# A hybrid encoder layer: the first embedding projection moved into the front stage, routing's order of work changed

## Chip, cores and metric

One core of a Trainium2 chip runs the whole kernel in one launch. The metric is the device time in microseconds; the median of three runs is given for the kernel before.

## What is computed

One layer over 1056 tokens (1024 of a prompt, 32 of a running stream), model width 1024, everything in float32:

```
h  = rmsnorm(x, g_mix);  z = h @ w_in                    # 1024 -> 1536
a  = z_a * sigmoid(z_g);  c = silu(layernorm(dwconv31(a)))
x  = x + concat(c @ w_pw + b_pw, pool_mix(z_u)) @ w_out
h2 = rmsnorm(x, g_ffn)
group = argmax(h2 @ w_rg);  e1, e2 = top 2 of the group's 8 experts (h2 @ w_re)
moe = sum over e1, e2: gate_e * ((silu(h2 @ w_gate[e]) * (h2 @ w_up[e])) @ w_down[e])
x  = x + moe
x  = x + sigmoid(rmsnorm(x, g_ple) @ w_ple_gate + b) * (p @ w_ple_proj)   # p: 256 -> 1024
y  = rmsnorm(x, g_final)
```

There are 32 experts of 6 MB of weights each. The product `p @ w_ple_proj` depends on nothing else in the layer, so it can be computed anywhere before the last stage.

## The kernel before

The 1056 tokens and a gap of 32 rows make nine tiles (`TILES` = 9) of 128 rows. The kernel is written in Bass: every engine has its own hand-written program with semaphores, in four blocks: `front`, `routing`, `experts`, `embedding_gate`. A block ends with a barrier of all engines; below such a place is called a joint.

**`front`** computes everything up to `h2` and the router's logits. Its end is a pipeline over tiles: TensorE's `out_products(t, h)` (the product with `w_out`, half h of the columns), VectorE's `add` and `norm2`, TensorE's `turn2(t, j)` (transposes of `h2`), ScalarE's `h2t_leave`, TensorE's `route(t)` (the logits). SP stores `x2_rows` and `h2_rows` for each tile and, before the last tile, issues the loads of the first expert's six weight pieces (GU 0 to 3, DOWN 4 and 5, 1 MB each) into `raw`. SP's last waits are for the landing of all stores. `p_rows` and `proj_w` are loaded earlier in this stage.

**`routing`** has two strands. VectorE works through a chain of small dependent steps (choice of experts, one-hots, ranks, places in the list of work items), with matmuls of TensorE between them: `count_tokens` and `rank_tokens` after `to_rank` 1, small ones after `to_rank` 2 and 3, and `list_tokens(0)` and `(1)`, which turn `row_parts[0]`, `row_parts[1]` and `at_item` into the list of tokens of each item. GpSimd makes tables of numbers and at the end issues the first gather of tokens. Beside this runs the embedding projection: TensorE's `turn_p(t)` transposes `p`, ScalarE's `leave_p(t)` copies the result out of PSUM, TensorE's `project(t)` multiplies (two halves of two matmuls, each recorded as two), ScalarE's `leave_proj(t)` copies both halves out, and SP's `store(t)` writes them to `proj_rows`. `ps_proj` holds one tile, so a half of `project(t)` waits until `leave_proj(t - 1)` has taken that half; `p_t` and `ps_pt` have two buffers. Tiles 0 to 4 (`LATE` = 5) are projected here, tiles 5 to 8 only turned. ScalarE also makes the six first weight copies (`first_copy`, from `raw` to `work`) and two small Exp steps. SP ends the block with

```
sp.wait_ge(projected, 2 * LATE)
sp.wait_ge(p_turned, T)
for s in (0, 1, 2):
    load_piece(sp, S, s, 1, 1, slice(1, 2))
```

which is two DMA issues for each of three pieces of the second expert.

**`experts`** loops over 49 items (an item is up to 64 tokens of one expert). For each: `gate_up` (32 matmuls), `turn_x` of the next item, `down` of the item before, `turn_hid`. ScalarE and VectorE copy the next expert's pieces from `raw` to `work` when the expert changes; SP loads two experts ahead, as `w_ready` allows, and at the end loads what the last stage needs, ending with `g_final_rows`. **`embedding_gate`** combines, gates and normalises.

Helper lines that the profile shows: L106 is a weight copy, L90 and L94 its loads, L1574 `project`, L1564 `turn_p`, L1519 `leave_p`, L1527 `leave_proj`, L1458 `store`, L1596 `list_tokens`, L1639 VectorE's two-input steps in `routing`, L1303 `route`, L1297 `turn2`, L1938 `turn_x`, L1951 `gate_up`.

## Time and profile before

| | us |
|---|---|
| median of three runs | 1168.76 (1167.81 to 1170.07) |
| profiled execution, its own time | 1167.64 |
| its span, first to last instruction | 1165.9 |
| `front` ends, `routing` begins | 409.8 |
| first transpose of `experts` | 447.95 |
| TensorE busy | 1075.2 (92%) |
| VectorE, ScalarE, GpSimd busy | 510.8, 510.0, 281.1 |
| mean granted TensorE clock | 0.97 |

Positions are microseconds from the start of the span. The profile is of one execution; the durations in it are compared with that execution's own time, and its distance to the median is kept in mind. The granted clock is a share of 2.4 GHz: 0.50 is 1.2 GHz, and a value between the two levels in a short stretch means that it changed within it. "<-" at the end of a row names what ended the idle time before an instruction.

### The profile page before, as it was taken

Reading aid. Unit: us, or ns where it says so; the run is one execution under the profiler, and the core shown is the slowest. Engines: PE = TensorE matmul, PEld = TensorE weight load, DVE = VectorE, ACT = ScalarE, POOL = GpSimd, SP = SyncE. Lnnn points to the kernel's source line nnn. Section 1 sums busy time; section 2 is a strip of 40 time slices with the busy share of each in tenths; the row PEclk is TensorE's granted clock in tenths of the full one; section 3 lists DMA queues with packets and bytes.
Section 4 is the critical chain, followed back from the end, with each engine's and each line's share of the span. In section 5 each row is a group of like instructions: output and inputs, shape, how many; then the busy total and the mean of one; then the engine's idle time right before and its main releaser. Section 6 shows DMA issues by size and latency. Waiting matters only on the chain. (4 is left out here: it accounts for less than half of the span.)

```text
span 1165.9 us, 17839 instructions
## 1 busy us (share of the span) xinstructions
PE 1075.2 (92%) x5269; PEld 616.0 (53%) x5270; DVE 510.8 (44%) x660; ACT 510.0 (44%) x690; POOL 281.1 (24%) x303
## 2 busy tenths in 40 slices
PE   2799996889999886999999999999999999969996
PEld 2799995778888642333333333333333333328885
DVE  4457999996222171213213212311312312356886
ACT  4343554766222144335435535534633535423432
POOL 1045886687000011111011101111101111023320
PEclk9899999899999878999999999999999999989999
DMA  7041753212113748999999999999999999965541
GB/s 226 1 136 55 200 140 139 66 63 96 60 73 132 283 177 320 397 380 337 395 397 358 399 397 384 374 396 396 361 395 397 361 397 397 402 248 172 208 145 41
DMA packets 149297, 300.32 MB, mean 258 GB/s; under 512 B 12032, under 2 KB 42784, under 8 KB 149259
## 3 DMA queue, kind: packets, MB, share of 16 engines
q1 hardware_dynamic: 134907, 264.69, 61.8%
q0 software_dynamic: 6512, 22.29, 5.5%
q10 hardware_dynamic: 7840, 12.85, 2.9%
q8 instruction: 22, 0.36, 0.1%
q14 instruction: 16, 0.13, 0.0%
HBM read 261.72 MB, written 38.06 MB: 257 GB/s over the span
## 5 line engine op out<-in xcount | busy, mean ns | idle before, releaser
L1951 PE MATMUL ps_gate_up<-weights,x_turned 128*64 128x512 f32 x1568 | 349.6, 598 | 1.4 <-issue 0.7
L106 ACT COPY weights<-raw_weights 128x2048 f32 (+1 forms) x99 | 186.1, 1899 | 102.8 <-issue 46.8
L1951 PEld LDWEIGHTS ps_gate_up<-weights,x_turned 128*64 128x64 f32 x1568 | 109.5, 137 | 206.9 <-issue 205.8
L106 DVE COPY weights<-raw_weights 128x2048 f32 x93 | 114.6, 1233 | 217.8 <-PE ps_gate_up L1951 85.8
L1964 PE MATMUL ps_y<-weights,h_turned 128*64 128x512 f32 x784 | 179.0, 598 | 0.9 <-ACT h_turned L1871 0.9
L431 POOL TENSOR_TENSOR conv_pool_taps<-conv_pool_taps,tap_product 128x448 f32<-128x448 f32 (+1 forms) x88 | 134.7, 1531 | 41.3 <-ACT tap_product L518 31.7
L1911 DVE TENSOR_TENSOR hidden<-ps_gate_up,act_gate 128x256 f32<-128x256 f32 x49 | 20.8, 425 | 222.9 <-ACT act_gate L1862 214.8
L115 POOL COPY token_ids<-item_tokens 128x1 int32 (+1 forms) x48 | 8.8, 183 | 446.9 <-PE ps_x L1938 446.9
L850 DVE SCALAR_TENSOR_TENSOR taps_bank<-a_ext,par,taps_bank 128x640 f32<-128x640 f32 (+1 forms) x128 | 101.6, 794 | 3.3
L1964 PEld LDWEIGHTS ps_y<-weights,h_turned 128*64 128x64 f32 x784 | 52.2, 136 | 93.3 <-issue 92.2
L518 ACT ACTIVATE tap_product<-a_ext,par 128x448 f32<-128x448 f32 (+1 forms) x104 | 75.9, 740 | 50.4 <-POOL conv_pool_taps L431 38.9
L118 POOL DMA_INDIRECT x_tokens<-h_rows,token_ids x48 | 61.3, 1276 | 37.7 <-POOL token_ids L115 37.7
L63 PE MATMUL bank<-w_out_hi,o_hi 128*128 128x512 f32 (+1 forms) x144 | 59.4, 412 | 0.6 <-DVE o_lo L916 0.6
L63 PE MATMUL ps_gate<-ple_hi,h3t_hi 128*128 128x512 f32 x144 | 57.8, 401 | 0.0
L64 PE MATMUL bank<-w_out_lo,o_hi 128*128 128x512 f32 (+1 forms) x144 | 57.5, 399 | 0.0
L65 PE MATMUL bank<-w_out_hi,o_lo 128*128 128x512 f32 (+1 forms) x144 | 57.5, 399 | 0.0
L65 PE MATMUL ps_gate<-ple_hi,h3t_lo 128*128 128x512 f32 x144 | 56.8, 394 | 0.0
L64 PE MATMUL ps_gate<-ple_lo,h3t_hi 128*128 128x512 f32 x144 | 56.4, 392 | 0.0
L1862 ACT ACTIVATE act_gate<-ps_gate_up 128x256 f32<-128x256 f32 x49 | 18.6, 379 | 84.7 <-PE ps_gate_up L1951 84.7
L1849 ACT ACTIVATE y_tile<-ps_y 128x512 f32<-128x512 f32 x49 | 29.2, 595 | 51.9 <-PE ps_y L1964 51.8
L1871 ACT ACTIVATE h_turned<-ps_h 128x256 f32<-128x256 f32 x49 | 18.8, 384 | 65.1 <-issue 65.1
L1938 PEld LDWEIGHTS ps_x<-ident,x_tokens 128*128 128x128 f32 x196 | 20.9, 142 | 43.8 <-issue 43.8
(285 smaller groups left out, 1546.0 us busy)
## 6 DMA issues: line engine op xcount, KB each, us to landing
raw_weights<-w_exp_gate SPq DMA_DIRECT2D x128, 512.0 KB
raw_weights<-w_exp_up SPq DMA_DIRECT2D x128, 512.0 KB
raw_weights<-w_exp_down SPq DMA_DIRECT2D x64, 1024.0 KB
y_rows<-y_tile ACTq DMA_DIRECT2D x98, 128.0 KB, 5.4
y_rows<-zero_rows SPq DMA_DIRECT2D x16, 512.0 KB, 6.2
x_rows<-x_tile SPq DMA_DIRECT2D x9, 512.0 KB, 2.7
h_rows<-h_tile SPq DMA_DIRECT2D x9, 512.0 KB, 2.9
mixer<-x_rows SPq DMA_DIRECT2D x9, 512.0 KB, 4.5
```

The source lines that it names most:

```text
L63: pe.matmul(out, x_hi, w_hi, start=start, stop=False)
L64: pe.matmul(out, x_hi, w_lo, start=False, stop=False)
L65: return pe.matmul(out, x_lo, w_hi, start=False, stop=stop)
L106: copy(S.work[s][:, :], raw).then_inc(S.w_ready[s], 1)
L118: pool.indirect_dma_start(out=S.x_tokens[:, :], out_offset=None, in_=S.h2_rows.rearrange("t (h n) -> (t h) n", h=SIDES), in_offset=bass.In ...
L431: pool.tensor_tensor(out, out, of(j + 1), ALU.add).then_inc(product_added, 1)
L518: act.activation(product[j % 2][:, 0:cols.stop - cols.start], a_ext[c][:, cols.start + k:cols.stop + k], ACT.Copy, scale=S.par[:, c, k:k + ...
L850: dve.scalar_tensor_tensor(conv[:, c, cols] if last else acc, src, w, acc, ALU.mult, ALU.add)\
L1849: act.activation(y[:, :], ps_y[:, :], ACT.Copy).then_inc(y_left, 1)
L1938: last = pe.transpose(ps_x[:, k, :], x[:, k * P:(k + 1) * P], S.ident[:, :])
L1951: last = pe.matmul(ps_gu[side[j], :, :], x_t[:, c, side[of]], w[:, :, share(D_EXP, j)], start=(k == 0), stop=(k == KD - 1))
L1964: last = pe.matmul(ps_y[side[j], :], h_t[:, c, side[of]], w[:, share(D, j)], start=(k == 0), stop=(k == KE - 1))
```

## The change

- `front`: TensorE turns tile 0 of `p` (`first_turn`) and projects it in two halves (`first_project`), placed among the last `out_products`, `turn2` and `route`. ScalarE copies the results out (`first_p_leave`, `first_proj_leave`), into buffers that are free by then. SP stores the tile and waits for its landing at the block's end.
- `routing`: tile 0 is gone from all engines, with the counts of the semaphores shifted. TensorE's order is new: one tile and a half are projected ahead of the counts, the second half of tile 2 after them, `list_tokens(0)` and `(1)` and the product with `owners` come ahead of `project(4)`. ScalarE's weight copies and leaves are interleaved in another way. The product `row_parts[1]` is computed by GpSimd, after a new semaphore, and no longer by VectorE.
- The loads of pieces 0, 1, 2 of the second expert are issued at the start of `experts` and no longer at the end of `routing`. SP then waits for the stores of the projections before it loads `late_w`.

The diff, with its context cut:

```diff
@@ -230,6 +230,7 @@
         gain2 = gain
+        p_first, proj_first = pool_sum[:, 0:PLE].rearrange("p (k n) -> p k n", n=P), sq[:, :, :].rearrange("p k n -> p (k n)")
         x, xn = S.room[0:DEEP], S.room[DEEP:2 * DEEP]
@@ -239,6 +240,7 @@
         ln_bank, var_bank = taps_bank[:, 0:2 * P], taps_bank[:, 2 * P:2 * P + 2]
+        p_bank, proj_bank = taps_bank[:, 512:512 + PLE].rearrange("p (k n) -> p k n", n=P), o_bank
 
@@ -261,6 +263,8 @@
         h2_turned, h2t_ready = sem("h2_turned"), sem("h2t_ready")
+        first_p_turned, first_p_left, first_projected, first_proj_left = (
+            sem(f"first_{n}") for n in ("p_turned", "p_left", "projected", "proj_left"))
         x2_stored, h2_stored = [sem(f"x2_stored{j}") for j in range(3)], [sem(f"h2_stored{j}") for j in range(2)]
@@ -370,10 +374,13 @@
                             load_piece(sp, S, s, 0, 0, slice(0, 1))
+                sp.wait_ge(first_proj_left, 2)
+                sp.dma_start(S.proj_rows[0:P, :], proj_first).then_inc(S.proj_stored[0], 16)
                 for j in range(3):
...
                     sp.wait_ge(h2_stored[j], 16 * ((TILES + 1 - j) // 2))
+                sp.wait_ge(S.proj_stored[0], 16)
 
@@ -573,6 +580,17 @@
                        .then_inc(h2t_ready, 1)
+
+                def first_p_leave():
+                    act.wait_ge(conv_done, 2 * KC)
+                    act.wait_ge(first_p_turned, 1)
+                    act.activation(p_first, p_bank, ACT.Copy).then_inc(first_p_left, 1)
+
+                def first_proj_leave(h):
+                    act.wait_ge(first_projected, h + 1)
+                    if h == 0:
+                        act.wait_ge(var_sum, PARTED)
+                    act.activation(proj_first[:, half(h)], proj_bank[h][:, :], ACT.Copy).then_inc(first_proj_left, 1)
 
@@ -779,10 +797,13 @@
                 square2(7)
+                first_p_leave()
                 h2t_leave(7, 0)
...
                 h2t_leave(7, 1)
+                first_proj_leave(0)
                 h2t_leave(8, 0)
+                first_proj_leave(1)
                 h2t_leave(8, 1)
@@ -1297,6 +1318,22 @@
 
+                def first_turn():
+                    pe.wait_ge(S.p_loaded, 16)
+                    pe.wait_ge(taps_left, 2 * KC)
+                    for k in range(PLE // P):
+                        last = pe.transpose(p_bank[:, k, :], S.p_rows[:, 0, k * P:(k + 1) * P], S.ident[:, :])
+                    last.then_inc(first_p_turned, 1)
+
+                def first_project(h):
+                    pe.wait_ge(S.proj_w_loaded, 16)
+                    pe.wait_ge(first_p_left, 1)
+                    pe.wait_ge(o_left, BLOCKS * PARTED)
+                    for k in range(PLE // P):
+                        last = pe.matmul(proj_bank[h][:, :], p_first[:, k, :], S.proj_w[:, k, half(h)],
+                                         start=(k == 0), stop=(k == PLE // P - 1))
+                    last.then_inc(first_projected, 1)
+
                 def route(t):
@@ -1374,11 +1411,14 @@
                 out_products(8, 0)
+                first_turn()
                 turn2(7, 0)
...
                 turn2(7, 1)
+                first_project(0)
                 route(7)
                 turn2(8, 0)
+                first_project(1)
                 turn2(8, 1)
@@ -1448,23 +1488,20 @@
         to_place, placed = sem("to_place"), sem("placed")
+        row_ready, parts_ready = sem("row_ready"), sem("row_parts_ready")
         bc = lambda ap, shape: ap.to_broadcast(shape)
...
                 def store(t):
-                    sp.wait_ge(proj_left, 2 * t + 2)
+                    sp.wait_ge(proj_left, 2 * t)
                     sp.dma_start(S.proj_rows[t * P:(t + 1) * P, :], proj_out[t % SLOTS][:, :]).then_inc(proj_stored[t % SLOTS], 16)
...
                     load_piece(sp, S, s, 1, 1, slice(1, 2))
-                for t in range(LATE):
+                for t in range(1, LATE):
                     store(t)
-                sp.wait_ge(projected, 2 * LATE)
-                sp.wait_ge(p_turned, T)
-                for s in (0, 1, 2):
-                    load_piece(sp, S, s, 1, 1, slice(1, 2))
                 sp.wait_ge(S.y_cleared, 16 * (ITEMS * BLOCK // P - EXPERTS * BLOCK // P) + 16)
@@ -1506,15 +1543,19 @@
                                    base=0, pattern=[[1, P]], channel_multiplier=-1).then_inc(made, 1)
+                pool.wait_ge(row_ready, 1)
+                pool.tensor_tensor(row_parts[1][:, :, :], at_row[:, :, :],
+                                   bc(tile_ids[:, :, :].rearrange("p k t -> p (k t)").unsqueeze(2), [P, 2 * T, BLOCK]), ALU.mult)\
+                    .then_inc(parts_ready, 1)
                 pool.wait_ge(S.tokens_ready, 1)
...
                 def leave_p(t):
-                    act.wait_ge(p_turned, t + 1)
-                    if 2 <= t < LATE:
-                        act.wait_ge(projected, 2 * t - 2)
+                    act.wait_ge(p_turned, t)
+                    if 3 <= t < LATE:
+                        act.wait_ge(projected, 2 * t - 4)
                     out = p_t[t % 2][:, :, :] if t < LATE else S.p_late[:, t - LATE, :, :]
@@ -1523,33 +1564,32 @@
                         half = slice(h * 512, (h + 1) * 512)
-                        act.wait_ge(projected, 2 * t + h + 1)
+                        act.wait_ge(projected, 2 * t + h - 1)
                         act.activation(proj_out[t % SLOTS][:, half], ps_proj[:, half], ACT.Copy).then_inc(proj_left, 1)
...
                 first_copy = lambda s: copy_piece(act, S, 0, s, None, on_act=True)
-                leave_p(0)
                 leave_p(1)
-                leave_proj(0)
                 leave_p(2)
...
                 leave_proj(1)
-                leave_p(3)
                 act.wait_ge(to_exp, 1)
...
                 first_copy(GU[1])
+                leave_p(3)
+                first_copy(GU[2])
+                leave_p(4)
                 leave_proj(2)
-                leave_p(4)
-                first_copy(GU[2])
-                leave_proj(3)
                 leave_p(5)
                 first_copy(GU[3])
+                leave_p(6)
                 first_copy(DOWN[0])
+                leave_proj(3)
                 first_copy(DOWN[1])
...
                 act.activation(m2[:, :], m2[:, :], ACT.Exp).then_inc(exp_ready, 1)
+                leave_p(7)
                 leave_proj(4)
-                for t in range(6, T):
-                    leave_p(t)
+                leave_p(8)
 
@@ -1558,17 +1598,17 @@
                         pe.wait_ge(sample_loaded, 16)
-                    if t >= 2:
-                        pe.wait_ge(p_left, t - 1)
+                    if t >= 3:
+                        pe.wait_ge(p_left, t - 2)
                     for k in range(KP):
...
 
-                def project(t):
-                    pe.wait_ge(p_left, t + 1)
-                    for h in range(2):
-                        if t > 0:
-                            pe.wait_ge(proj_left, 2 * t + h - 1)
+                def project(t, halves=(0, 1)):
+                    pe.wait_ge(p_left, t)
+                    for h in halves:
+                        if t > 1:
+                            pe.wait_ge(proj_left, 2 * t + h - 3)
                         for k in range(KP):
@@ -1597,34 +1637,34 @@
 
-                turn_p(0)
                 turn_p(1)
-                pe.wait_ge(proj_w_loaded, 16)
-                project(0)
                 turn_p(2)
                 project(1)
+                project(2, (0,))
                 pe.wait_ge(made, 6)
...
                 rank_tokens()
+                turn_p(3)
                 pe.wait_ge(to_rank, 2)
...
                 pe.matmul(ps_expert, expert_row[0:E, :], at_order[0:E, :], start=True, stop=True).then_inc(ranked, 1)
-                for t in range(2, 4):
-                    turn_p(t + 1)
-                    project(t)
+                project(2, (1,))
+                turn_p(4)
+                project(3)
                 turn_p(5)
+                turn_p(6)
                 pe.wait_ge(to_place, 1)
                 list_tokens(0)
+                pe.wait_ge(parts_ready, 1)
+                list_tokens(1).then_inc(placed, 1)
                 pe.wait_ge(to_place, 2)
-                list_tokens(1).then_inc(placed, 1)
+                pe.matmul(flat_tot[:, 0:ITEMS + 1], owners[:, :], S.ident[:, 0:ITEMS + 1], start=True, stop=True).then_inc(placed, 1)
+                turn_p(7)
                 project(4)
-                pe.wait_ge(to_place, 3)
-                pe.matmul(flat_tot[:, 0:ITEMS + 1], owners[:, :], S.ident[:, 0:ITEMS + 1], start=True, stop=True).then_inc(placed, 1)
-                for t in range(6, T):
-                    turn_p(t)
+                turn_p(8)
 
@@ -1711,6 +1751,7 @@
                    ALU.is_equal)
+                dve.sem_inc(row_ready, 1)
                 ts(row_parts[0][:, :, :], at_row[:, :, :], own_ids[:, :], None, ALU.mult)
@@ -1721,8 +1762,6 @@
                    ALU.is_equal)
-                dve.sem_inc(to_place, 1)
-                tt(row_parts[1][:, :, :], at_row[:, :, :], bc(flat(tile_ids[:, :, :]), [P, 2 * T, BLOCK]), ALU.mult)
                 dve.sem_inc(to_place, 1)
@@ -1792,6 +1831,10 @@
 
+                for s in (0, 1, 2):
+                    load_piece(sp, S, s, 1, 1, slice(1, 2))
+                for j in range(SLOTS):
+                    sp.wait_ge(S.proj_stored[j], 16 * len(range(j, LATE, SLOTS)))
                 sp.dma_start(S.late_w[:, :, :], ple_proj).then_inc(S.proj_w_loaded, 16)
@@ -2322,6 +2365,7 @@
         S.ple_hi_ready, S.ple_split = (whole.enter_context(nc.semaphore(n)) for n in ("ple_hi_ready", "ple_split"))
+        S.proj_stored = [whole.enter_context(nc.semaphore(f"proj_stored{j}")) for j in range(SLOTS)]
         S.w_experts = (i["w_exp_gate"], i["w_exp_up"], i["w_exp_down"])
@@ -2360,7 +2404,6 @@
             blocks = lambda w: w[0].rearrange("(k p) n -> p k n", p=P)
-            S.proj_stored = [whole.enter_context(nc.semaphore(f"proj_stored{j}")) for j in range(SLOTS)]
             routing(nc, S)
```

## Rows read from the trace of the kernel before

**Rows 1.** Windows: busy us (instructions) of PE, PEld, DVE, ACT, POOL, clock, DMA share, GB/s.

```profile
540.00:560.00 20.00, 20.00 (x94) 6.61 (x94) 7.71 (x8) 11.13 (x13) 3.45 (x4) 1.00 0.86 315
```

**Rows 2.** Waits of SP, 1000 to 1045: us in total, times, longest.

```profile
SPq L1790 <- DMA g_final_rows<-g_final: 15.7, 1, 15.7
```

**Rows 3.** Windows of one us in the expert loop, columns as rows 1.

```profile
542.00:543.00 1.00, 1.00 (x8) 0.29 (x4) 0.00 (x0) 0.99 (x1) 0.59 (x1) 1.00 0.00 0
```

**Rows 4.** Timeline, PE, 445 to 475: start, us, instruction, idle before and its releaser.

```profile
447.95 1.11 PE L1938 MATMUL ps_x<-ident,x_tokens 128*128 128x128 f32 x4 [4.64 <-PEq L1452]
449.74 9.37 PE L1951 MATMUL ps_gate_up<-weights,x_turned 128*64 128x512 f32 x32 [0.69 <-ACT x_turned L1844]
...
462.86 7.09 PE L1951 MATMUL ps_gate_up<-weights,x_turned 128*64 128x512 f32 x32 [0.72 <-issue]
```

**Rows 5.** Waits of SP, 399 to 412.

```profile
SPq L376 <- DMA h_rows<-h_tile: 8.5, 1, 8.5
```

**Rows 6.** Timeline, PE, end of the front stage.

```profile
398.69 2.67 PE L1303 MATMUL ps_route<-w_route,h_t 128*128 128x36 f32 x16 [2.00 <-ACT h_t L574]
...
404.81 3.63 PE L1303 MATMUL ps_route<-w_route,h_t 128*128 128x36 f32 x16 [0.69 <-ACT h_t L574]
```

**Rows 7.** Timeline, SP, end of routing.

```profile
443.38 0.38 SPq L90 DMA_DIRECT2D raw_weights<-w_exp_gate  x1
...
446.09 0.47 SPq L90 DMA_DIRECT2D raw_weights<-w_exp_up  x1
447.01 0.37 SPq L1795 DMA_DIRECT2D late_ple_proj<-w_ple_proj  x1
```

**Rows 8.** Timeline, ACT, end of routing.

```profile
435.64 0.38 ACT L1519 ACTIVATE p_late<-ps_pt 128x256 f32<-128x256 f32 x1
435.90 5.50 ACT L106 COPY weights<-raw_weights 128x2048 f32<-128x2048 f32 x3
...
441.40 1.08 ACT L1527 ACTIVATE projected<-ps_proj 128x512 f32<-128x512 f32 x2
...
443.35 0.38 ACT L1519 ACTIVATE p_late<-ps_pt 128x256 f32<-128x256 f32 x1 [0.32 <-PE ps_pt L1564]
```

**Rows 9.** Timeline, PE, routing.

```profile
415.95 3.60 PE L1574 MATMUL ps_proj<-ple_proj,p_turned 128*128 128x512 f32 x8
419.48 0.38 PE L1580 MATMUL ps_tot<-ones_b,onehot_sum 128*32 128x1 bf16 x9
...
424.76 0.69 PE L1564 MATMUL ps_pt<-ident,p_rows 128*128 128x128 f32 x2
...
434.94 0.38 PE L1564 MATMUL ps_pt<-ident,p_rows 128*128 128x128 f32 x2
```

**Rows 10.** Window at the end of the front stage, columns as rows 1.

```profile
404.00:408.50 4.50, 3.75 (x17) 3.49 (x16) 0.00 (x0) 0.60 (x1) 0.00 (x0) 0.50 1.01 408
```

**Rows 11.** Timeline, DVE, routing.

```profile
416.73 0.46 DVE L1639 TENSOR_TENSOR onehot_sum<-onehot 128x288 bf16<-128x288 f32 x1
...
426.58 1.36 DVE L1639 TENSOR_TENSOR at_row<-iota_lanes,row_in_item 128x1152 bf16<-128x1152 f32 x1
...
432.06 1.36 DVE L1639 TENSOR_TENSOR row_token_part<-at_row,tile_half_rows 128x1152 bf16<-128x1152 bf16 x1 [0.15 <-DVE at_item L1639]
```

**Rows 12.** Windows of one us around changes of the clock, columns as rows 1.

```profile
399.00:400.00 1.00, 1.00 (x10) 1.00 (x9) 1.00 (x1) 0.00 (x0) 0.00 (x0) 0.89 1.06 391
423.00:424.00 1.00, 0.23 (x1) 0.23 (x2) 0.78 (x4) 0.00 (x0) 0.00 (x0) 0.83 0.11 45
430.00:431.00 1.00, 1.00 (x3) 0.40 (x2) 0.90 (x4) 0.00 (x0) 0.00 (x0) 0.75 0.00 0
```

**Rows 13.** Groups by form, POOL: busy us, mean ns, idle before.

```profile
L431 POOL TENSOR_TENSOR conv_pool_taps<-conv_pool_taps,tap_product 128x640 f32<-128x640 f32 x40 | 73.6, 1839 | 24.8 <-ACT tap_product L518 20.5
```

**Rows 14.** The line of the projection's stores (L1458): from issue to landing.

```profile
DMA to landing us min/median/max: 2.6/2.9/3.9
```

**Rows 15.** Timeline, DVE, first item of the expert loop.

```profile
456.00 1.23 DVE L106 COPY weights<-raw_weights 128x2048 f32 x1 [13.08 <-PE ps_gate_up L1951]
```

## The prediction

> **What bounds the kernel now.** I read the page first: TensorE is busy for 92% of the span, so the question is what it still waits for. Busy time by stretch shows the expert loop as a solid block of TensorE at full clock; from 540 to 560 us it has no idle time while the DMA share falls to 0.86, so there the weights wait for buffers and TensorE sets the pace [rows 1]. Therefore whatever moves the first item of the loop moves everything behind it. The loop's own end waits for a load, not for TensorE: SP sat 15.7 us on the last gain row [rows 2]. Those loads queue behind expert weights that were issued as buffers came free, so this end too follows TensorE's pace. The DMA queue still empties at 542 us, so a late start of the weight stream is made good there, up to about 4 us [rows 3].
>
> So the change is worth what it does to the start of TensorE's first expert transpose, 447.95 us [rows 4]. Two joints stand before it. At the end of the front stage SP waited 8.5 us for the last `h_rows` store, until 409.2 us, while TensorE's last `route` ended at 408.4: the store set the joint [rows 5, 6]. At the end of `routing`, ScalarE's last copy ended at 443.73 but SP was still issuing six weight loads, from 443.38 to 446.56; SP's next DMA came at 447.01 and TensorE followed 1.39 us after SP's last issue [rows 4, 7, 8].
>
> **The front stage.** It gains, on TensorE, `first_turn` (2 transposes) and two half projections (2 matmuls, 4 records each), on ScalarE three copies, on SP one 512 KB store and two waits. `first_project(0)` fits the 2.0 us that TensorE idled before `route(7)` [rows 6]: 4 records of 0.44 us (the eight of one tile took 3.53 us, first start to what follows) are 1.8 us [rows 9]. `first_project(1)` is 1.8 us more between the last two turns. With that gap gone the clock should stay at 2.4 GHz; before, `route(8)` ran at 1.2 GHz in 3.63 us. I get TensorE's end at about 407, before SP's wait. ScalarE's copies lie in idle time. The store does not: the queue ran at 408 GB/s until 408.5 us with the weights in it, and the new store, issued at about 404, goes behind them [rows 10]. 0.524 MB / 408 GB/s = 1.3 us. `routing` begins 1.3 us later, at about 411.1: **+1.3**. Behind SP's wait for `first_proj_left` stand only the block's closing waits. On ScalarE `h2t_leave(7, 0)` stands behind `first_p_leave`, and on TensorE `out_products(8, 1)` behind `first_turn`: 0.3 us, which the earlier end covers. Bounds: 0 if the store lands in the shadow, +3 if the clock falls anyway and the whole TensorE tail runs at 1.2 GHz.
>
> The Trainium skill ("DMA: Bandwidth & Descriptors", Anatomy of one DMA) fits one DMA on GpSimd's path with a fixed 2.0 us plus bytes at 436 GB/s. By it this store would take 3.2 us, be down by 407.6, and the term would be 0. The 8.5 us wait for a store of the same size speaks against it here.
>
> **`routing`, up to the counts.** Before, TensorE reached `count_tokens` at 419.48 after two tiles (16 records), though VectorE had released it at 417.2 [rows 9, 11]. After, it does one tile and a half (12 records): four records of 0.44 less, 1.8 us, against the 1.3 us of later start (which assumes that the clock rises as long after the start as before; a later rise costs 0.44 for each record still at 1.2 GHz). Counts at about 419.1: **-0.4**. VectorE's release would be at 418.5, so no more is to be had here than -1.0.
>
> **From the counts to `turn_p(5)`.** VectorE's chain from the counts to the masks is unchanged; TensorE, free for the next turn at 424.8 before, is so at 424.4 after. Before, it then did 16 records and three turns and had turned tile 5 at 435.32 [rows 9]. After, it does 4 (`project(2, (1,))`), a turn, 8 (`project(3)`), a turn. The first four run at 1.2 GHz, 0.88 each: 3.5 us, to 427.8, the turn to 428.4. Then comes a wait that before did not have: `project(3)` needs `proj_left` 4 and so `leave_proj(2)`, which ScalarE runs only behind `leave_p(4)`, which waits for that turn: 0.4 + 0.6 us, to 429.4. In before the clock fell at 423.7 and rose at 430.5 (by the means 0.83 and 0.75 of the us in which it changed), 5.7 us after TensorE's restart [rows 12]; the same 5.7 us give 430.1. One record at 0.88 and seven at 0.44, then the turn: tile 5 turned at 433.5. **-1.8** with the -0.4 above in it. If the pause delays the rise past `project(3)`, it is 8 x 0.44 = 3.5 us more at most; if the clock never falls, 1.8 + 0.4 less.
>
> VectorE no longer does the 1.36 us multiplication; GpSimd does. Its nearest row is 1.84 us for 640 columns, 2.9 ns each, so 1152 columns are 3.3 us, from 427.6 to 431 [rows 11, 13]. TensorE comes to `list_tokens` at 433.8, the other operand is ready at 431.9 - 0.4: both hidden with over 2 us of cover; past it, each us that the table is late delays `list_tokens`, and then the first gather. Behind GpSimd's new wait stands only that gather. The two share no instruction with the rest, but if they slowed each other by half on the 3.3 us, the cover still holds. Nothing is gained either, since TensorE, not VectorE, was late there.
>
> **ScalarE's tail.** Before, from `leave_p(5)` at 435.64: three weight copies in 5.50, Exp, `leave_proj(4)` 1.08, three more `leave_p`: 8.1 us to 443.73 [rows 8]. After, the same three copies still stand behind `leave_p(5)` (the earlier copies moved only within ScalarE's idle time), and `leave_proj(3)`, 1.1 us, now stands among them: 9.4 us, from 433.6 to 443.0. But `project(4)` now waits for that `leave_proj(3)`: `leave_p(5)`, copy, `leave_p(6)`, copy, half a leave is 4.9 us, so it starts at 438.5, after TensorE has idled some 3 us. All at 2.4 GHz it ends at 442.0 and costs nothing; all at 1.2 GHz it takes 7.0 us, ends at 445.5, and the end is 446.4. The rows show the clock falling after pauses of 2 to 3 us [rows 12]; I take the middle, 5.1 us: ScalarE ends at **444.6**.
>
> **SP.** The six issues move behind the joint. The last event before it is 444.6 in place of 446.56: **-2.0**. That is the whole of the gain: 446.0 for the first transpose. The loads then start at 445.1, 1.7 us later than now, and `late_ple_proj` and all later weights with them. The new wait for `proj_stored` is over before SP reaches it (3.2 us of issues against 2.9, the median landing of such a store) [rows 14]. What covers the shift is that the copy of the second expert's second piece waited for TensorE and not for data [rows 15], and later the empty queue at 542 us. I price it at 0; without that cover it is up to the 1.7 us.
>
> **The first item's clock.** `gate_up` of item 0 took 9.37 us against 7.09 of item 1, because TensorE had been idle for 7 us [rows 4]. Now it pauses for 2 to 3 us. The bound is -2.3; I take 0, since such pauses did drop the clock elsewhere.
>
> **The sum.** -2.0, against the profiled execution's 1167.64 (span 1165.9 and 1.7 around it): 1165.6. That execution is 1.1 us under the median of the three runs, which gives **1166.8** for a median.
>
> **Rivals.**
> 1. The clock holds through `routing`. For it: the pauses are shorter than those that dropped it. Against: shorter ones did drop it too. `project(2, (1,))` -1.8, `project(3)` -0.4, `project(4)` -1.6 more, part of the first item's 2.3: about -5, 1163.8. Chance 0.15.
> 2. The front's store is hidden: -1.3 more, 1165.5. For it: the quickest such store landed in 2.6 us [rows 14]. Against: the 8.5 us. Chance 0.10.
> 3. Slower. ScalarE's order makes `project(3)` and `project(4)` wait, and TensorE runs both at 1.2 GHz: 3.1 us and 1.8 us on 444.6 give 449.5, against 446.56: +2.9, 1171.7. It decides from the point where these two cost over 2.0 us more than I assume. Chance 0.12.
> 4. The gain is given back by the weights: loads 1.7 us later against a first item 2.0 us earlier, and a copy of the second expert waits; or the front costs 3 instead of 1.3. 1168.7. Chance 0.13.
>
> The forecast (a gain of 0.3 to 3.5 us) has 0.50. 0.2% is 2.34 us, about what this kernel's measurement can tell from no change. Faster by more than that: rivals 1 and 2 and a third of the forecast, 0.42. Slower: most of rival 3, 0.10. The rest, 0.48, is within it. Range: 1163.6 (rival 1) to 1170.8 (rival 3 in part); beyond it lies less than 0.2.
>
> **What would show it.** SP's wait at the end of the front is on `proj_rows` and ends near 410.4. `count_tokens` starts at 419 to 420. TensorE pauses about 1 us before `project(3)` and about 3 us before `project(4)`. The last event before the second joint is ScalarE's `leave_p(8)`, 443 to 446. The six loads are issued right after it. TensorE is never starved in the loop; the whole difference is there at its first transpose. I am wrong if the joint comes after 447, if the front's end doesn't move, or if TensorE waits for weights in the first three items.

## The result, and the profile after

| | median us | runs | ratio to before [95%] |
|---|---|---|---|
| before | 1169.80 | 20 | |
| changed kernel | 1176.71 | 20 | 1.0048 [1.0034, 1.0061] |

The change makes the kernel slower by 0.5%. (The ratio is estimated from all runs and is not the quotient of the two medians, which lie 6.9 us apart; it makes 5.6 us of 1170.) The profiled execution of the changed kernel took 1172.44 us, span 1170.7 against 1165.9. That is +4.8, a little under the 5.6. The loss is complete at the third item: its `gate_up` starts at 479.11 instead of 474.42, +4.69, and from there on both kernels run alike (11.56 us per item, and TensorE busy for all of the 520 us from 480 to 1000 in both).

The front stage of the changed kernel: the last `route` in TensorE's timeline, then SP's waits as [rows 5].

```profile
404.99 1.97 PE L1340 MATMUL ps_route<-w_route,h_t 128*128 128x36 f32 x16 [0.74 <-ACT h_t L581]
```

```profile
SPq L382 <- DMA h_rows<-h_tile: 4.9, 1, 4.9
...
SPq L383 <- DMA proj_rows<-conv_sq: 1.1, 1, 1.1
```

`route(8)` takes 1.97 us instead of the 3.63 of [rows 6]: the clock holds. SP now waits for `h_rows` and 1.1 us more for the new store, which took 6.5 us from its issue at 404.47 to its landing.

`routing` on TensorE, as [rows 9], in order of time:

```profile
412.61 7.87 PE L1614 MATMUL ps_proj<-ple_proj,p_turned 128*128 128x512 f32 x12
420.41 0.38 PE L1620 MATMUL ps_tot<-ones_b,onehot_sum 128*32 128x1 bf16 x9
...
425.68 3.78 PE L1614 MATMUL ps_proj<-ple_proj,p_turned 128*128 128x512 f32 x4
...
430.95 5.50 PE L1614 MATMUL ps_proj<-ple_proj,p_turned 128*128 128x512 f32 x8 [1.05 <-ACT projected L1568]
436.29 0.60 PE L1604 MATMUL ps_pt<-ident,p_rows 128*128 128x128 f32 x4
...
441.59 5.30 PE L1614 MATMUL ps_proj<-ple_proj,p_turned 128*128 128x512 f32 x8 [2.82 <-ACT projected L1568]
446.73 0.38 PE L1604 MATMUL ps_pt<-ident,p_rows 128*128 128x128 f32 x2
```

Both foreseen waits are there, 1.05 us before `project(3)` and 2.82 us before `project(4)`. What wasn't foreseen is the length of the blocks: 12 records in 7.87 us, and 5.50 us for `project(3)`. The windows as [rows 12] show why. First the rise of the clock after the restart at the block's beginning (409.82 before, 411.48 after), before and after, then the second rise of the changed kernel:

```profile
412.00:413.00 1.00, 1.00 (x3) 0.45 (x2) 0.93 (x3) 0.00 (x0) 0.79 (x6) 0.50 1.04 404
413.00:414.00 1.00, 1.00 (x3) 0.41 (x2) 0.86 (x5) 0.00 (x0) 0.46 (x2) 0.79 1.04 406
```

```profile
416.00:417.00 1.00, 1.00 (x2) 0.34 (x1) 0.86 (x5) 0.57 (x1) 0.00 (x0) 0.50 0.91 360
417.00:418.00 1.00, 1.00 (x3) 0.53 (x2) 0.90 (x4) 0.03 (x1) 0.00 (x0) 0.71 1.02 389
...
433.00:434.00 1.00, 1.00 (x2) 0.46 (x2) 0.90 (x4) 0.00 (x0) 0.00 (x0) 0.50 0.41 168
434.00:435.00 1.00, 1.00 (x3) 0.27 (x1) 0.85 (x1) 0.00 (x0) 0.00 (x0) 0.68 0.00 0
```

Before, the clock rose in the window from 413, about 3.6 us after the restart; after, in the one from 417, about 6.1 us after. The second time it rose 5.7 us after the restart before [rows 12], and 9.0 us after it now (`project(2, (1,))` starts at 425.68, the rise is at 434.6), though TensorE was busy but for the 1.05 us and short gaps.

The end of `routing`: ScalarE as [rows 8], SP as [rows 7].

```profile
436.70 0.38 ACT L1560 ACTIVATE p_late<-ps_pt 128x256 f32<-128x256 f32 x1 [5.41 <-PE ps_pt L1604]
436.99 1.89 ACT L106 COPY weights<-raw_weights 128x2048 f32<-128x2048 f32 x1
...
440.84 1.10 ACT L1568 ACTIVATE projected<-ps_proj 128x512 f32<-128x512 f32 x2
...
447.42 0.38 ACT L1560 ACTIVATE p_late<-ps_pt 128x256 f32<-128x256 f32 x1
```

```profile
448.32 0.38 SPq L90 DMA_DIRECT2D raw_weights<-w_exp_gate  x1
...
451.62 0.40 SPq L1838 DMA_DIRECT2D late_ple_proj<-w_ple_proj  x1
```

ScalarE closes the block at 447.80; the six loads follow it. The first items, as [rows 4, 15]: TensorE, then VectorE's and ScalarE's copies of the second expert's pieces, and last the copy of ScalarE in the kernel before.

```profile
449.88 0.65 PE L1981 MATMUL ps_x<-ident,x_tokens 128*128 128x128 f32 x4 [2.76 <-issue]
451.21 8.78 PE L1994 MATMUL ps_gate_up<-weights,x_turned 128*64 128x512 f32 x32 [0.69 <-ACT x_turned L1887]
...
465.24 0.62 PE L2014 MATMUL ps_h<-ident,hidden 128*128 128x128 f32 x2 [4.66 <-DVE hidden L1954]
...
466.39 8.25 PE L1994 MATMUL ps_gate_up<-weights,x_turned 128*64 128x512 f32 x32 [0.53 <-issue]
```

```profile
458.36 1.23 DVE L106 COPY weights<-raw_weights 128x2048 f32 x1 [13.12 <-DMA raw_weights<-w_exp_up]
...
461.14 1.90 ACT L106 COPY weights<-raw_weights 128x2048 f32 x1 [4.53 <-DMA raw_weights<-w_exp_up]
```

```profile
457.60 1.90 ACT L106 COPY weights<-raw_weights 128x2048 f32 x1 [2.02 <-PE ps_gate_up L1951]
```

Before, both copies waited for TensorE. Now both wait for data. ScalarE's stands ahead of the activation of item 0 in its program, so `turn_hid` of item 0 waits 4.66 us instead of 2.01. It starts 4.10 us after that copy, as before (4.11), and 15.36 us after the block's first transpose instead of 13.76: +1.60. TensorE comes out of that pause at the lower clock: `gate_up(1)` has a mean granted clock of 0.86 instead of 1.00 and takes 8.25 us instead of 7.09, +1.16. These two are the whole growth from the first transpose to `gate_up(2)`, 2.76 us.

VectorE in `routing` before and after, as [rows 11], and GpSimd after:

```profile
427.98 0.52 DVE L1641 TENSOR_SCALAR row_token_part<-at_row,own_half_rows 128x1152 bf16<-128x1152 bf16 x1
```

```profile
429.02 2.42 DVE L1681 TENSOR_SCALAR row_token_part<-at_row,own_half_rows 128x1152 bf16<-128x1152 bf16 x1 [0.16 <-DVE at_row L1679]
```

```profile
429.01 2.12 POOL L1547 TENSOR_TENSOR row_token_part<-at_row,tile_half_rows 128x1152 bf16<-128x1152 bf16 x1 [13.84 <-DVEq L1754]
```

VectorE's step took 0.52 us and now takes 2.42, and ends 0.31 us after GpSimd's. `list_tokens` still starts as soon as TensorE is free (436.82; VectorE's last operand for it was ready at 434.85).

### The profile page after: what moved, and what is told of

Its sections match the earlier page's. It is cut to its first block and busy times, and to the rows that moved or that the text cites. A ratio compares the mean times of both kernels' runs of the same rounds, so it can differ in the third digit from the quotient of the medians.

```text
span 1170.7 us, 17842 instructions
## 1 busy us (share of the span) xinstructions
PE 1076.9 (92%) x5269; PEld 614.8 (53%) x5270; DVE 511.7 (44%) x659; ACT 509.6 (44%) x690; POOL 283.7 (24%) x304
## 5 line engine op out<-in xcount | busy, mean ns | idle before, releaser
L1981 PEld LDWEIGHTS ps_x<-ident,x_tokens 128*128 128x128 f32 x196 | 20.6, 141 | 41.9 <-issue 41.9
```

## The experiments

Executions differ by up to 5.5 us ahead of these stages, so stretches are compared within a trace. The table cuts each profiled execution at six points on TensorE: the start of `route(6)` (382.88 in before), of the first transpose of `routing` and of `count_tokens`, the end of the last `turn_p`, the start of the first transpose of `experts` and of `gate_up(2)`. "after_again" and "front_tile_again" are second measurements of the changed kernel and of the front tile alone. Us:

| kernel | to routing | to counts | to last turn | to experts | to gate_up(2) | sum | ratio to before |
|---|---|---|---|---|---|---|---|
| before | 26.9 | 9.7 | 23.8 | 4.6 | 26.5 | 91.5 | 1 |
| changed | 27.9 | 8.9 | 26.7 | 2.8 | 29.2 | 95.5 | 1.0048 |
| after_again | 28.0 | 8.8 | 26.6 | 2.8 | 30.9 | 97.1 | 1.0030 |
| before_loads_late | 26.8 | 9.7 | 23.9 | 1.7 | 31.6 | 93.7 | 1.0028 |
| before_front_tile | 28.0 | 7.6 | 22.3 | 4.6 | 26.2 | 88.7 | 0.9979 |
| front_tile_again | 28.3 | 7.6 | 22.5 | 4.5 | 27.6 | 90.4 | 0.9973 |
| before_rows_gpsimd | 27.0 | 9.6 | 23.8 | 4.8 | 26.5 | 91.6 | 1.0004 |
| after_order_back | 28.3 | 7.6 | 22.3 | 1.7 | 29.6 | 89.4 | 1.0003 |
| after_loads_early | 28.5 | 8.5 | 26.4 | 5.9 | 26.0 | 95.3 | 1.0040 |
| after_leaves_first | 28.0 | 8.5 | 21.8 | 5.0 | 30.5 | 93.8 | 1.0012 |
| after_half_back | 28.5 | 7.6 | 28.8 | 2.8 | 29.8 | 97.4 | 1.0026 |
| front_tile_pieces | 28.6 | 7.6 | 23.8 | 2.7 | 27.5 | 90.3 | 0.9997 |
| front_tile_copies | 28.5 | 7.6 | 20.6 | 4.6 | 26.7 | 88.1 | 0.9969 |
| front_tile_pieces_copies | 28.1 | 7.6 | 20.7 | 3.8 | 27.5 | 87.6 | 0.9965 |

The sums are one execution each; the ratios decide, over 7 to 20 runs of a kernel against 20 to 35 of before. 0.001 of ratio is 1.2 us.

**The three parts apart.** First the late loads alone, on the kernel before:

```diff
-                sp.wait_ge(projected, 2 * LATE)
-                sp.wait_ge(p_turned, T)
-                for s in (0, 1, 2):
-                    load_piece(sp, S, s, 1, 1, slice(1, 2))
...
             @block.sync
             def _(sp):
 
+                for s in (0, 1, 2):
+                    load_piece(sp, S, s, 1, 1, slice(1, 2))
+                for j in range(SLOTS):
+                    sp.wait_ge(S.proj_stored[j], 16 * len(range(j, LATE, SLOTS)))
                 sp.dma_start(S.late_w[:, :, :], ple_proj).then_inc(S.proj_w_loaded, 16)
```

> The kernel before with one edit: the loads of the second expert's pieces 0 to 2 are issued at the start of experts and no longer at the end of routing (with the waits for the stored projections, as in the change). Theory L (loads): the second item starts when these pieces have landed and been copied; in the changed kernel its turn_hid came 16.9 us after the first of these issues. The joint would end at 444.2, the issues start at 444.4 and not 443.4, TensorE's first transpose come 2.5 us earlier; turn_hid of item 0 near 461.3 against 461.7: -0.5 us, or up to +1, and a wait for data on VectorE's or ScalarE's weight copy. Theory S (start of TensorE, that of the prediction): -2.5 us.

Measured 1.0028 [1.0014, 1.0041]: slower by itself, by 3.3 us, which is more than either theory gave. `experts` starts 2.9 us sooner after the last turn, and `gate_up(2)` comes 5.1 us later after that start. VectorE and ScalarE in the trace of this kernel, then TensorE:

```profile
456.43 1.23 DVE L106 COPY weights<-raw_weights 128x2048 f32 x1 [11.36 <-DMA raw_weights<-w_exp_up]
```

```profile
459.04 1.90 ACT L106 COPY weights<-raw_weights 128x2048 f32 x1 [4.22 <-DMA raw_weights<-w_exp_up]
```

```profile
463.15 0.50 PE L1971 MATMUL ps_h<-ident,hidden 128*128 128x128 f32 x2 [4.44 <-DVE hidden L1911]
...
464.31 10.00 PE L1951 MATMUL ps_gate_up<-weights,x_turned 128*64 128x512 f32 x32 [0.67 <-issue]
```

The two copies start 10.3 and 12.9 us after the first load's issue (446.15); in the changed kernel it is 10.0 and 12.8. In before they started 12.6 and 14.2 us after it (443.38), held by TensorE. So the cover was 2.3 to 2.6 us for the one and 1.3 to 1.4 us for the other, while the loads moved 3.5 us later against the first transpose (issued 4.57 us ahead of it before, 1.04 us here). 3.5 less 1.3 is 2.2 us, and by so much later does `turn_hid` of item 0 come after the first transpose: 15.96 us instead of 13.76. Against the last turn it comes 0.7 us sooner (17.7 us behind it instead of 18.4), as theory L had it. So waiting for the weights alone would only have eaten most of the 2.9 us gained at the joint. What makes this trace longer is `gate_up(1)` behind the wait of 4.44 us: a mean granted clock of 0.70 instead of 1.00, and 10.00 us instead of 7.09.

Is the lower clock there a consequence of the longer wait? In all six traces with late loads `turn_hid` of item 0 waits 3.3 to 4.7 us and `gate_up(1)` takes 8.2 to 10.0. In the eight with early loads it waits 2.0 us, and `gate_up(1)` takes 7.09 in five and 8.78 in three. So the longer wait goes with the lower clock, but it isn't the only thing that does.

Then the front tile alone: the change with the loads at the end of `routing` again, the second row table on VectorE, and the order of before on TensorE and ScalarE, without tile 0. Beside the diff of `front`, what differs from before is

```diff
-                for t in range(LATE):
+                for t in range(1, LATE):
                     store(t)
...
-                leave_p(0)
                 leave_p(1)
-                leave_proj(0)
                 leave_p(2)
...
-                turn_p(0)
                 turn_p(1)
-                pe.wait_ge(proj_w_loaded, 16)
-                project(0)
                 turn_p(2)
                 project(1)
```

> The kernel before with one part of the change: tile 0 of the projection is turned, projected and stored in the front stage and gone from routing; order, loads and the row table otherwise as before. Theory O (the new order in routing and the late loads make the loss): routing begins 1.0 to 1.3 us later because SP waits for one more store, TensorE gets that back by one tile less before the counts: within 1 us of the kernel before. Theory F (the front part makes the loss): +1.3 us or more, the whole shift kept up to the first transpose.

> The kernel before with the front tile alone once more (0.9979 [0.9965, 0.9993] the first time; with the pieces issued apart it came to 0.9997 on another chip). If the gain is real: 0.997 to 0.999, the last turn near 443, the first transpose near 447.5. If it was chance: 0.9995 to 1.001.

Measured 0.9979 [0.9965, 0.9993], and 0.9973 [0.9955, 0.9992] the second time: 2.5 and 3.2 us faster, more than theory O's "within 1 us". The front stage gets 1.1 and 1.4 us longer, and `routing` 3.6 and 3.5 us shorter up to the last turn: 2.1 us before the counts, where TensorE had been late, and 1.5 and 1.4 behind them.

The loads of the changed kernel put back (the reverse of the first diff), all else as changed:

> The changed kernel with the six issues of the second expert's pieces put back to the end of routing. Theory L: they start 0.9 us earlier (right after the last turn), the first transpose comes 2 us later, and turn_hid of item 0 moves by -0.9 to 0: as the changed kernel or up to 1 us less, so about +5 us on the kernel before. Theory S: 2.1 us more than the changed kernel, about +8.

Measured 1.0040 [1.0023, 1.0058], +4.7 us, theory L's number and not the +8 of theory S. The late loads cost and gain nothing that shows here: TensorE waits 5.9 us at the joint instead of 2.8, and then 26.0 instead of 29.2 us pass to `gate_up(2)`. That leaves the order of `routing`, which was undone with the late loads and GpSimd's table kept:

```diff
                 project(1)
-                project(2, (0,))
                 pe.wait_ge(made, 6)
...
-                turn_p(3)
                 pe.wait_ge(to_rank, 2)
...
-                project(2, (1,))
-                turn_p(4)
-                project(3)
-                turn_p(5)
-                turn_p(6)
+                for t in range(2, 4):
+                    turn_p(t + 1)
+                    project(t)
+                turn_p(5)
```

and so on, with ScalarE's leaves and copies in the order of before as well.

> The changed kernel with TensorE's and ScalarE's order in routing put back to that of before (without tile 0); front tile, row table on GpSimd and late loads stay. Theory O: the last turn comes 2 to 3 us earlier than in the changed kernel, and the time falls by as much, to +2 to +4 us on the kernel before. If the order is innocent, nothing changes: +6.

Measured 1.0003 [0.9986, 1.0019], better than the +2 to +4 us of theory O. So the new order costs some 0.3 to 0.45% with the loads late (1.0030 or 1.0048 against 1.0003) and 0.6% with them early (1.0040 against 0.9979 and 0.9973; GpSimd's table is the other difference there, and costs nothing, see below). In the old order the late loads cost 0.24 to 0.3% (1.0003 against 0.9979 and 0.9973), as they did on the kernel before. From the counts to the last turn it is 22.3 us in the old order without tile 0, and 26.4 to 26.7 in the new one.

The two late rises of the clock part here. The first comes 4.8 to 6.4 us after `routing`'s restart in all eleven traces with the front tile, the old order among them, and 3.4 to 3.8 us after it in the three without; so it goes with the front tile and not with the order. What differs ahead of it: with the front tile the clock holds until after `route(8)` (it falls at 407.3 in the changed kernel, at 399.8 in before). It costs most where a tile and a half stand ahead of the counts. The second goes with the order. After the counts the granted clock stays at 0.50 for 10.2 us in all four traces with the order as changed (also with ScalarE's leave moved, below), for 6.8 us with the half tile put back, and in the old order with the front tile for 3.4 us in five traces of six (6.8 in the other).

**Within the new order.** ScalarE's leave of `project(3)` moved up:

```diff
                 leave_p(5)
+                leave_proj(3)
                 first_copy(GU[3])
                 leave_p(6)
                 first_copy(DOWN[0])
-                leave_proj(3)
                 first_copy(DOWN[1])
```

> The changed kernel with ScalarE's leave_proj(3) straight behind leave_p(5), ahead of the copies of pieces 3 and 4. Theory A (project(4) is late because this copy out of PSUM stands behind two weight copies): TensorE's 2.8 us pause before project(4) goes, its 8 records take about 3.7 us instead of 5.3, it ends near 442.5 instead of 446.9; ScalarE then sets the joint by its own 9.5 us of work behind tile 5, which ends near 446.2 instead of 447.8: -1.6 us, ratio 1.0048 - 0.0014 = 1.0034. Rival B (the lateness comes from further up, the counts and tile 5): the pause goes but the joint moves by less than 0.5 us, ratio 1.0045 or more.

Measured 1.0012 [0.9998, 1.0026], clear of the changed kernel's first ratio and just overlapping the one of its second measurement (1.0030 [1.0011, 1.0049]). The pause is gone and the eight records take 3.60 us:

```profile
437.44 1.08 ACT L1568 ACTIVATE projected<-ps_proj 128x512 f32<-128x512 f32 x2
```

```profile
438.82 0.39 PE L1604 MATMUL ps_pt<-ident,p_rows 128*128 128x128 f32 x2
439.05 3.60 PE L1614 MATMUL ps_proj<-ple_proj,p_turned 128*128 128x512 f32 x8
```

The last turn comes 4.9 us sooner after the counts. Of that 2.2 us are lost at the joint, which ScalarE now closes (445.80), as theory A had it. The first transpose still comes 3.1 us sooner after `routing`'s start, more than the 1.6 reckoned; behind it 1.2 us are lost again, with `gate_up(0)` and `gate_up(1)` at 9.89 and 9.26 us, 2.1 us over the changed kernel's. That the sum falls by 1.7 us, near theory A's 1.6, is luck. The ratio fell by more than that (by 2 to 4 us) and is better than either theory gave.

The half tile put back behind the counts:

```diff
-                project(2, (0,))
...
-                project(2, (1,))
+                project(2)
```

> The changed kernel with project(2) whole behind the counts, no half of it before them. Theory A (the half tile ahead of the counts delays VectorE's chain, and the four records cost the same anywhere): from routing's start to the counts 7.6 us instead of 8.9; the four records come back after the counts at 0.4 to 0.9 us each, so that tile 5 is turned within 0.7 us of where it was: ratio 1.004 to 1.006. Rival B (VectorE's chain decides): the joint and all behind it 1.3 us earlier, ratio 1.0037.

Measured 1.0026 [1.0008, 1.0044], under what either theory gave, but overlapping both values of the changed kernel. The first step is as expected (7.6 us to the counts). In the profiled execution tile 5 was turned 16.8 us after the counts (437.7, against 16.2), so about half of the 1.3 us that was won ahead of them went behind them; what makes this trace the longest of all is `project(4)`, 6.72 us where it was 5.30, at the lower clock nearly throughout (0.50 until 449.0):

```profile
442.72 6.72 PE L1614 MATMUL ps_proj<-ple_proj,p_turned 128*128 128x512 f32 x8 [2.83 <-ACT projected L1568]
```

Between the two theories this run doesn't decide.

The changed kernel itself again, on another chip than its first 20 runs:

> The changed kernel itself once more, on the chip of the next three, because its variants came to 1.0012 and 1.0026 on a chip where it had not been timed. If its loss is its own and not that chip's: ratio 1.0034 to 1.0061 again. If chips differ: a ratio near 1.003, and then the variants stand closer to it than they seem.

Measured 1.0030 [1.0011, 1.0049]. Slower again; the two intervals overlap from 1.0034 to 1.0049. Whether the chips differ stays open, so its variants are held against both values.

**GpSimd's table alone**, on the kernel before:

```diff
+                pool.wait_ge(row_ready, 1)
+                pool.tensor_tensor(row_parts[1][:, :, :], at_row[:, :, :], ..., ALU.mult)\
+                    .then_inc(parts_ready, 1)
...
-                tt(row_parts[1][:, :, :], at_row[:, :, :], bc(flat(tile_ids[:, :, :]), [P, 2 * T, BLOCK]), ALU.mult)
```

> The kernel before with only the second row table made on GpSimd. Theory A (hidden): GpSimd's multiplication takes about 2.1 us, VectorE's one beside it about 2.4 instead of 0.5 us, at_item and the gate weights about 0.5 us later or earlier in sum (1.9 us longer one, 1.4 us less work), list_tokens stays where TensorE reaches it; ratio within 0.0012 of 1. Rival B (VectorE's delay reaches the lists): list_tokens waits, and the last turn is up to 1.9 us later, ratio 1.0016.

Measured 1.0004 [0.9990, 1.0018]: nothing, with all stretches as in before. VectorE's step is again 2.42 us long, and `list_tokens` starts at 435.11 (435.25 before).

```profile
427.98 2.42 DVE L1647 TENSOR_SCALAR row_token_part<-at_row,own_half_rows 128x1152 bf16<-128x1152 bf16 x1 [0.16 <-DVE at_row L1645]
```

**A better version.** Of the second expert's pieces only piece 1 needs both the last turn and the last projection: by the order and sizes of the buffers, piece 0's place holds `p_rows` of tiles up to 2 alone, piece 2's place `proj_w` alone, and piece 1's what is left of both. On the front tile alone, the loads were issued apart:

```diff
+                sp.wait_ge(p_turned, 2)
+                load_piece(sp, S, 0, 1, 1, slice(1, 2))
-                for t in range(1, LATE):
+                for t in range(1, LATE - 1):
                     store(t)
                 sp.wait_ge(projected, 2 * LATE - 2)
+                load_piece(sp, S, 2, 1, 1, slice(1, 2))
+                store(LATE - 1)
                 sp.wait_ge(p_turned, T - 1)
-                for s in (0, 1, 2):
-                    load_piece(sp, S, s, 1, 1, slice(1, 2))
+                load_piece(sp, S, 1, 1, 1, slice(1, 2))
```

> The kernel before with the first tile's projection in the front stage (the version that measured 0.9979), and the three pieces of the second expert's weights issued apart: piece 0 as soon as tile 2 is turned, piece 2 right after the last projection, piece 1 after the last turn. Theory A (SP's six issues after the last turn stand before the block's end, and the piece copies of item 1 wait for these loads): four of the six issues leave the tail; the first transpose comes 2.1 to 2.8 us after the last turn's end instead of 4.6, and everything behind is earlier by as much: about 1.9 us more, ratio 0.996 to 0.997; the copies of item 1 wait for TensorE. Rival B (the early transfers collide with the running stores and the pieces 3 to 5, or the joint is set by something else): the last turn comes later or the joint stays, ratio 0.998 as for the front tile alone, or worse.

Measured 0.9997 [0.9979, 1.0014]. The joint did shrink (2.7 us instead of 4.6) and the copies waited for TensorE, but the ratio shows no gain over the front tile (the intervals overlap, on different chips): rival B by the number, and in part by its mechanism, since the last turn came later, 23.8 us after the counts instead of 22.3. In the trace `project(2)` took 6.17 us instead of 5.30, and `gate_up(1)` 8.78. The second also happened once with the front tile alone (front_tile_again), so it isn't the pieces' doing for certain. Next, ScalarE's copies one place earlier, first on the front tile alone, then with the pieces apart as well:

```diff
                 leave_proj(1)
-                leave_p(3)
                 act.wait_ge(to_exp, 1)
                 act.activation(g4[:, :, :], g4[:, :, :], ACT.Exp).then_inc(exp_ready, 1)
                 first_copy(GU[1])
-                leave_proj(2)
-                leave_p(4)
+                leave_p(3)
                 first_copy(GU[2])
-                leave_proj(3)
-                leave_p(5)
+                leave_proj(2)
+                leave_p(4)
                 first_copy(GU[3])
+                leave_proj(3)
+                leave_p(5)
                 first_copy(DOWN[0])
```

> Front tile alone, and ScalarE's Exp and its weight copies one place earlier (Exp and piece 1 before leave_p(3), piece 2 before leave_proj(2), piece 3 before leave_proj(3)), so that two weight copies stand behind leave_p(5) instead of three. Theory A (ScalarE's work behind tile 5 holds up leave_p(6), turn 8 and the joint): turn 8 no longer waits 2.05 us, last turn and loads 1.3 to 1.9 us earlier, near 441.3, and the whole as much earlier: 1.3 us under the front tile alone, ratio about 0.001 lower than it. Rival B (the copies held back by leave_p(3), leave_proj(2) and (3) delay projections): the last turn moves by less than 0.5 us, same ratio as the front tile alone. Rival C: a shorter end of routing but a lower clock behind it, nothing left of the gain.

> The same, with piece 0 of the second expert loaded after tile 2's turn and piece 2 after the last projection, so that two issues stand behind the last turn. Theory A (joint and loads both earlier): first transpose near 444.5, 3 us before the front tile alone, ratio about 0.0025 lower than it, copies of item 1 waiting for TensorE. Rival C (the clock): with the pause at the joint only 2.7 us, the first item stays at 1.2 GHz or drops later, gate_up(0) and gate_up(1) together over 17 us as with the pieces apart alone (17.4), and half of the gain or more is lost.

Measured 0.9969 [0.9952, 0.9986] and 0.9965 [0.9949, 0.9981], against 0.9973 for the front tile alone on the same chip. Both are faster than before and than the changed kernel. Turn 8 waits 0.44 us instead of 2.05, and the last turn is 1.7 us sooner, as theory A of the first has it; but the ratios are only 0.0004 and 0.0008 lower (0.5 and 0.9 us), and their intervals can't tell the three apart. With both edits:

```profile
442.63 1.11 PE L1977 MATMUL ps_x<-ident,x_tokens 128*128 128x128 f32 x4 [3.83 <-issue]
...
456.85 8.78 PE L1990 MATMUL ps_gate_up<-weights,x_turned 128*64 128x512 f32 x32 [0.82 <-issue]
```

```profile
449.88 1.23 DVE L106 COPY weights<-raw_weights 128x2048 f32 x1 [10.70 <-PE ps_gate_up L1990]
```

The copy waits for TensorE; the joint is 3.83 us and not 2.7, its end held by nothing that the profile names. `gate_up(0)` and `gate_up(1)` took 8.56 and 8.78, 17.3 together, as rival C said, against 16.5 in before [rows 4]. It expected a ratio 0.0025 lower than the front tile alone or less than half of that; 0.0008 is the latter.

## Why the prediction was wrong

The forecast of 1166.8 was a gain of 2.0 us. In the profiled execution it is a loss of 4.8, and the median came out at 1176.7, above the range. Step by step, in the prediction's terms:

- **The front stage, +1.3: right.** 0.9 us in this trace, 0.9 to 1.7 in all eleven traces that have the store. The clock held in `route(8)`, TensorE ended at 406.96 (forecast 407), and the store set the joint. Rival 2 fell: the store took 6.5 us to land. By the Trainium skill ("DMA: Bandwidth & Descriptors", Anatomy of one DMA), whose fit is for GpSimd's path, an estimate for it is 3.2 us; this one ran on SP's queue with the weights in it, and the measurement decides.
- **Up to the counts, -0.4: wrong by 0.9.** From `routing`'s start it was 8.9 us and not 8.0. The bracket named the reason ("assumes that the clock rises as long after the start as before; a later rise costs 0.44 for each record"): it rose 6.1 us after and not 3.6. Every trace with the front tile has a rise that late (4.8 to 6.4 us): holding the clock through `route(8)` and keeping the 3.6 us behind it did not go together.
- **Counts to `turn_p(5)`, 14.4 us: wrong by 1.8.** It was 16.2. The first four records (3.78, forecast 3.5) and the wait of 1.05 (forecast 1.0) were right. The step that failed is "the same 5.7 us": the clock rose 9.0 us after the restart, in the middle of `project(3)`, which took 5.50 and not 4.0. The text had this as "If the pause delays the rise past `project(3)`, it is 8 x 0.44 = 3.5 us more at most"; 1.5 us of that came.
- **GpSimd's table, nothing: right in the sum,** wrong in both sizes. 2.12 us and not 3.3, and VectorE's step grew from 0.52 to 2.42. The cover held.
- **ScalarE's tail: right.** From tile 5 turned to ScalarE's end 11.2 us, forecast 11.1; the pause before `project(4)` 2.8, forecast some 3; the eight records 5.30, forecast 5.1. Only that the tail began later. But to accept the pause was to accept the order: the runs show that it costs. With that leave in front the ratio is 1.0012.
- **SP's six issues, -2.0: right in what it removes.** With the loads moved alone the joint is 2.9 us shorter.
- **The late loads at 0: the step that failed, and the largest single term.** The text set the loads' shift (1.7 us) and the first item's (2.0 us earlier) in different sentences, and gave 1.7 us as the bound. Against each other they move by the sum of both, 3.7 us. And the cover was taken for long because the copy shown in [rows 15] waited for TensorE; how long the data had been there was not asked. It was 2.6 us for that copy and 1.4 us for ScalarE's. In the changed kernel the loads moved 3.0 us against the first transpose (1.56 us ahead of it instead of 4.57); less the 1.4 that is 1.6, and `turn_hid` of item 0 comes 1.60 us later after the first transpose. That is under the 1.7 us of the bound, by luck: with the shift of 3.7 us that the forecast implied it would have been 2.3. What the text didn't price at all is the clock behind the longer wait, 1.16 us in `gate_up(1)`. Together 2.76. On the kernel before, the late loads alone cost 3.3 us by the ratio. In the changed kernel they only cancel against the shorter joint (1.0048 and 1.0030 with them, 1.0040 without), where the forecast took the shorter joint as its whole gain. Rival 4 named this mechanism and gave it 1168.7.
- **The first item's clock, 0.** `gate_up(0)` took 0.6 us less (8.78), which gained nothing, since TensorE then waited for the copy; `gate_up(1)` lost the 1.2 after the new pause.

The sum against the forecast's -2.0: front -0.4, counts +0.9, from there to tile 5 +1.8, ScalarE's tail +0.1, from ScalarE's end to the first transpose +0.7 (2.08 us instead of the 1.4 taken; the profile names nothing for it), the loads +2.76, and +0.76 us that this execution was late before the changed place. That makes +4.6, against the +4.69 seen. The two steps on the clock in `routing` make 2.7 us together, as much as the loads; and by the runs the order weighs more, since undoing it leaves 1.0003 and putting the loads back leaves 1.0040.

Two of the text's own signs of being wrong came true: ScalarE closed the joint at 447.80, after 447, and TensorE waited for weights in the first item.

Shown by runs: the late loads cost by themselves on the kernel before, the new order costs, the front tile gains, GpSimd's table does nothing. Shown in traces, and not by a run that changes it alone: that much of the late loads' price is the clock behind the wait. For part of the order, ScalarE's leave behind two copies, the run with it moved speaks, though not clear of noise against the second measurement. Of the rivals, 4 came with its mechanism and 3 in part: `project(3)` and `project(4)` took 1.7 us more than the forecast had, not the 4.9 of rival 3. Neither came near 1176.7. Rival 1 was summed wrong: its terms make 3.8 us on top of the forecast's 2.0, so 1163.0 or less and not 1163.8; the clock did not hold, and nothing hangs on it. Open: what the half tile ahead of the counts costs by itself, and why the clock rises later after the restart, the first time with the front tile and the second time in the new order.

## What to carry to other kernels

When a load and its user move in opposite directions, add the two shifts, and compare the sum with how long the data lay there before its use (issue to use, against issue to use where the same use waits for data), not with who ended the wait. Then ask what the longer wait does to the clock of the work behind it: here that was nearly as much again. A copy out of PSUM on which the next matmul waits belongs ahead of copies that only fill time. A list of good edits in one change hides that some are bad: here one part alone gains 0.2 to 0.3%, and the others take back more than twice that.

## What the hardware showed that was not expected

- VectorE's `tensor_scalar` over 1152 bf16 columns took 2.42 us instead of 0.52 when GpSimd's two-input operation had started 0.01 us before it (twice, in two kernels), and ended 0.3 us after GpSimd's 2.12. That looks like being stopped, not slowed. The Trainium skill has such a case ("SBUF — State Buffer", Who interferes with whom): against a VectorE instruction in a two-port mode, who issues first gets the shared port pair for the whole instruction, and the other is fully blocked. 2.12 + 0.52 would be 2.64; the trace agrees within 0.2 us. No row shows which mode VectorE was in.
- The granted clock rose 3.6 us after `routing`'s restart in before, and 6.1 us after it in the changed kernel; after the counts 5.7 and 9.0 us. Two executions of the same kernel differed in `gate_up(1)` by 1.7 us (7.09 and 8.78, the front tile alone; 8.25 and 9.99, the changed kernel). A forecast that moves work across such a rise should carry it as a range of that size.
